# 64 bytes more between the contraction tiles of an expert's x, in a two-layer encoder trunk on one core

## The reference

```python
def moe_swiglu(h, w_router, w_gate_e, w_up_e, w_down_e):
    logits = (xt @ w_router).astype(jnp.float32)
    top_val, top_idx = lax.top_k(logits, TOP_K)          # TOP_K = 2 of 8
    gates = jax.nn.softmax(top_val, axis=-1)
    ...
    hg = lax.ragged_dot(xs, w_gate_e, sizes)             # 1024 -> 3584, by expert
    hu = lax.ragged_dot(xs, w_up_e, sizes)
    ys = lax.ragged_dot(jax.nn.silu(hg) * hu, w_down_e, sizes)   # 3584 -> 1024
    ys = ys * gates.reshape(-1)[order][:, None].astype(ys.dtype)
    out = jnp.zeros_like(xt).at[tok].add(ys)
```

## Time and profile before

| | us |
|---|---|
| median of 3 runs | 3622.34 |
| lowest, highest | 3621.78, 3625.7 |
| span of the profiled execution, first to last instruction | 3620.2 |
| TensorE busy in it | 3532.9 |
| DVE busy | 1803.5 |
| ACT busy | 1539.2 |

### The profile page before, as it was taken

How to read it: one execution, slowest core, us unless ns; L and a number is a source line. 1 busy time by engine, 2 the same in 40 slices (tenths; PEclk the granted TensorE clock), 3 DMA queues, 4 the chain that set the end, 5 groups by cost and what they waited for, 6 DMA issues and landing times. The chain is left out here.

```text
span 3620.2 us, 65480 instructions
## 1 busy us (share of the span) xinstructions
PE 3532.9 (98%) x24184; PEld 3219.3 (89%) x24184; DVE 1803.5 (50%) x2599; ACT 1539.2 (43%) x2207; POOL 205.3 (6%) x207
## 2 busy tenths in 40 slices
PE   8999899999999999979999999999999999999997
PEld 7888798888888889879899898998999999999997
DVE  5455543333333454465565565555655545545544
ACT  3445433332333342355454554544545444434433
POOL 1000000000000000040010010100100000000100
PEclk9999999999999999989999999999999999999999
DMA  5111332333223332256575565655655545544543
GB/s 190 37 49 39 140 94 93 93 93 117 93 93 99 121 95 67 101 190 220 184 236 193 193 230 186 231 186 190 231 194 194 191 157 177 193 162 158 183 159 124
DMA packets 158035, 540.68 MB, mean 149 GB/s; under 512 B 23480, under 2 KB 23520, under 8 KB 157920
## 3 DMA queue, kind: packets, MB, share of 16 engines
q1 hardware_dynamic: 129440, 467.72, 39.8%
q0 software_dynamic: 23872, 62.99, 5.0%
q10 hardware_dynamic: 4608, 8.39, 0.6%
HBM read 515.54 MB, written 45.48 MB: 155 GB/s over the span
## 5 line engine op out<-in xcount | busy, mean ns | idle before, releaser
L302 DVE TENSOR_TENSOR wl<-wraw,wh 128x1024 fp32r<-128x1024 f32 x884 | 1082.5, 1225 | 1322.0 <-ACT wh L298 1321.1
L298 ACT ACTIVATE wh<-wraw 128x1024 fp32r<-128x1024 f32 x884 | 934.2, 1058 | 1148.7 <-PE ps L315 1146.3
L315 PE MATMUL ps<-exh,wh 128*128 128x240 f32 (+3 forms) x3584 | 1019.3, 284 | 6.7 <-DVE wl L302 5.9
L315 PE MATMUL ps<-exl,wh 128*128 128x240 f32 (+3 forms) x3584 | 1018.8, 284 | 0.0
L315 PE MATMUL ps<-exh,wl 128*128 128x240 f32 (+3 forms) x3584 | 1018.7, 284 | 0.0
L315 PE MATMUL ps<-xs,wh 128*128 128x256 f32 (+1 forms) x3840 | 827.7, 323 | 2.4 <-DVE qAl L743 2.0
L315 PEld LDWEIGHTS ps<-exh,wh 128*128 128x128 f32 x3584 | 677.2, 189 | 7.4 <-issue 7.2
L315 PEld LDWEIGHTS ps<-exl,wh 128*128 128x128 f32 x3584 | 675.3, 188 | 0.2
L315 PEld LDWEIGHTS ps<-exh,wl 128*128 128x128 f32 x3584 | 675.2, 188 | 0.0
L315 PEld LDWEIGHTS ps<-xs,wh 128*128 128x128 f32 x3840 | 589.2, 188 | 76.2 <-issue 8.5
L315 PE MATMUL ps<-xs,wl 128*128 128x256 f32 (+1 forms) x1920 | 517.0, 321 | 0.0
(11 more groups left out here) (318 smaller groups left out, 3395.1 us busy)
## 6 DMA issues: line engine op xcount, KB each, us to landing
wraw<-in_w_expert SPq DMA_DIRECT2D x676, 512.0 KB, 3.3
wraw<-in_w_main SPq DMA_DIRECT2D x208, 512.0 KB, 3.5
hT<-in_xT POOLq DMA_DIRECT2D x2, 2048.0 KB, 10.1
h_d<-hT POOLq DMA_DIRECT2D x2, 2048.0 KB, 10.0
hT<-h_d POOLq DMA_DIRECT2D x2, 2048.0 KB, 13.9
xrow_d<-rows ACTq DMA_DIRECT2D x16, 256.0 KB, 2.0
hrow_d<-rows ACTq DMA_DIRECT2D x16, 256.0 KB, 3.9
yraw<-y_d POOLq DMA_DIRECT2D x4, 768.0 KB, 7.7
```

The lines of the kernel that those rows point to most:

```text
L298: act.activation(wh[:, j], wraw[:, j], ACT.Copy).then_inc(hi_done, 1)
L302: dve.tensor_tensor(wl[:, j], wraw[:, j], wh[:, j].bitcast(F32), ALU.subtract).then_inc(lo_done, 1)
L315: mm = pe.matmul(out[:, s], a, b[:, s], start=first and part == 0 and c == 0, stop=last and part == 2 and c + w == n)
```

## The change

The step from one contraction tile to the next of `exh` and `exl` grows by 16 floats (64 bytes) to 1600 bytes. The writes of ACT and DVE name columns 0 to 383 of it, as before. What lies behind the two tiles, and what the router keeps behind the items' tiles, moves up by 1024 bytes; the sets still fit. The whole diff:

```diff
--- before.py
+++ after.py
@@ -34,6 +34,7 @@
 NE = 8
 NG = 8
 CAP = 384
+SKEW = 16
 WIDTHS = (240, 256, 288, 304, 336, CAP)
 PIECES = -(-T // CAP)
 NCAND = PIECES * NE
@@ -171,7 +172,7 @@
         s3.close()
 
         s4 = ExitStack()
-        sb("under_items", [P, 2 * CAP + 2 * KD * CAP + 2 * F_EXP // P * CAP], F32, s4)
+        sb("under_items", [P, 2 * CAP + 2 * KD * (CAP + SKEW) + 2 * F_EXP // P * CAP], F32, s4)
         below = sb("below", [P, P], F32, s4)
         tokf = sb("tokf", [P, NT, 2], F32, s4)
         tokb = sb("tokb", [P, NT, 2], BF16, s4)
@@ -229,7 +230,7 @@
 
         s5 = ExitStack()
         mst = sb("mst", [P, 2, CAP], F32, s5)
-        exh, exl = (sb(n, [P, KD, CAP], F32R, s5) for n in ("exh", "exl"))
+        exh, exl = (sb(n, [P, KD, CAP + SKEW], F32R, s5) for n in ("exh", "exl"))
         mah, mal = (sb(n, [P, F_EXP // P, CAP], F32R, s5) for n in ("mah", "mal"))
         on = sb("on", [P, CAP // P, D], F32, s5)
         fgb = sb("fgb", [P, 512], F32, s5)
@@ -1802,12 +1803,12 @@
         def turn_x_act(act, it, banks=XT, ks=range(KD)):
             for k in ks:
                 act.wait_ge(xt_mm, 8 * it + (k + 1))
-                act.activation(exh[:, k], bank(banks[k], CAP), ACT.Copy, scale=gains[:, 3, k:k + 1]).then_inc(x_hi, 1)
+                act.activation(exh[:, k, 0:CAP], bank(banks[k], CAP), ACT.Copy, scale=gains[:, 3, k:k + 1]).then_inc(x_hi, 1)
 
         def turn_x_dve(dve, it, banks=XT, ks=range(KD)):
             for k in ks:
                 dve.wait_ge(x_hi, 8 * it + (k + 1))
-                dve.scalar_tensor_tensor(exl[:, k], bank(banks[k], CAP), gains[:, 3, k:k + 1], exh[:, k].bitcast(F32),
+                dve.scalar_tensor_tensor(exl[:, k, 0:CAP], bank(banks[k], CAP), gains[:, 3, k:k + 1], exh[:, k, 0:CAP].bitcast(F32),
                                          ALU.mult, ALU.subtract).then_inc(x_lo, 1)
 
         NF_E = F_EXP // P
```

## The result

The kernel after takes 3628.75 us, the median of 20 runs (3626.28 to 3634.76), beside 3622.97 us for the kernel before (3621.38 to 3628.37) on the same chip. The profiled execution spans 3627.4 us against 3620.2 us.

What follows compares the result with a forecast made beforehand. TensorE's own matmul stream was taken to bound the kernel. Matmuls, writes, later tiles and everything before the items were each put at 0, summing to 0, so the forecast stayed at 3622.3 us, range 3605 to 3638 us.

Steps and rivals of the forecast that it cites:

- What bounds the kernel, and how to price it: TensorE, busy 98% of the span, ends last; a matmul's price comes from starts in a stretch, 112.0 ns for 240 columns.
- The residue doesn't set the price: Stepping exh and exl through residues of 512 bytes costs TensorE's gate and up matmuls 0 ns, on three readings.
- The first: Two 256-column items at the same addresses cost 117.8 and 113.3 ns, so an address can't tell them apart.
- The second: wsh's 128-column matmul at distance 0 takes 111.4 ns, so up to 240 columns weight loads hide the moving operand's place.
- The third: 512 columns cost 233.4 ns in the dense layer and 234 in down halves, so turning the distance round changes nothing.
- Placement and the two ports: By the skill's separate TensorE read ports no placement of exh could matter, sum zero; the forecast wasn't rested on it.
- Rival (b): In gate and up products, changing distance at each k breaks the rhythm: slower, 3636 to 3643 us; chance 0.16.
- one sign of recognition: 288-column steps following k with a period of 24 matmuls, named as something that would make the prediction wrong.
- Rival (c): Excess is an address conflict that eight distances spread: half of the 32 us bound, 3606 us; chance 0.12.
- Rival (a): Rhythm drawn anew without any address; large flips 3611 us (chance 0.04) or 3630.5 us (0.02), small ones count as no change.
- (d): Change does what it says: exh and exl share a residue per k, eight in all; no effect, within no change's 0.66.
- Writes, waits, later tiles at 0: ACT's and DVE's writes (bound 2 us each), TensorE's waits for exl and tiles moved 1024 bytes were to add 0.

Runs made afterwards that it cites:

- x_plus64: Kernel before with exh and exl begun 64 bytes later at the old step, distance 0 modulo 256 from the weights; ratio 1.001.
- x_dist16: Kernel before with exh and exl meant to lie 16 bytes from the weights modulo 256, in fact 32 after the allocator's rounding; ratio 1.0027.
- dist0: Kernel before with 64 bytes put behind wl, so xs, mah and others get distance 0, exh and exl staying at 192; ratio 0.9986.
- half256: Kernel before with tiles 4 to 7 of exh and exl begun 256 bytes further, distance modulo 256 unchanged; ratio 0.9998.
- b_again: The kernel before without an edit, profiled once more; ratio 1.0005.
- rest1024: Kernel before with exh and exl kept and only the later tiles behind them moved by 1024 bytes; ratio 1.0.
- m1_micro: Separate kernel running only TensorE's product loop, other engines idle, at distances in 64-byte steps and the change's step; 256 columns 113.3 to 120.0 ns.
- m2_fine: The same TensorE-only loop at 16-byte distances, 512 columns included, and behind varied transposes or matmuls; 512 columns 226.7 to 236.7 ns.
- lead1: Kernel before with one more 256-column matmul at the start of each 256-column item; ratio 0.9998.

## Why the prediction was right or wrong

**What bounds the kernel, and how to price it: right.** TensorE's stream sets the end, the waits didn't move, and counting starts in a stretch finds the large terms of the 5.7 us.

**"The residue doesn't set the price": wrong, and this is the step that failed.** Each of the three readings was true, and none carried the conclusion. The first (same addresses, two prices) shows that something besides the address matters; I read it as showing that the address doesn't. The two micro kernels have both effects: for 256 columns at 192 bytes 113.3 and 117.8 ns are possible, at 0 only 120.0 was seen. In the kernel `x_plus64` has 120.0 ns, at distance 0, in both items. The second (wsh at distance 0 keeps the pace) is one price of 128 columns at one distance; no run here moves them to another, so it couldn't carry the conclusion that up to 240 columns the place is hidden. The 240 columns moved from 112.0 to 112.2 ns, 0.8 us in all, to 112.8 in `x_dist16` and to 113.3 in two items of `dist0`; I had named any such move as what makes the prediction wrong. The third (distance 192 against 64, and the earlier trace rows) compared two points where 233.3 occurs at both; distance 0, the one that would have told, with 226.7 ns, occurs for no 512-column product of the earlier trace rows.

**Placement and the two ports.** The loop alone, with ACT and DVE idle, has the prices of exh and exl in the kernel to 0.1 ns, and the same 512 columns cost 226.7 to 236.7 ns by distance. The Trainium skill, page SBUF — State Buffer, section "Who interferes with whom", gives TensorE separate read ports for the moving operand and the weights and has it wait for no other engine. The second half agrees with these runs. What I drew from the first half, that a placement can't matter, doesn't.

**Rival (b), slower by a broken rhythm: right in sign and in one sign of recognition, wrong in mechanism and size.** The steps do follow k with a period of 24. But `half256` shows that a jump in address costs nothing by itself, and 21 us became 5.7. Its price was taken between rhythms at one distance; what the change does is to replace one distance's price by about the mean of four, and that is a loss only where the one was the best: 6.7 us in the second 256 item.

**Rival (c), faster by spreading a conflict: true for 288 and 304 columns, 0.5 and 0.4 ns, 1.8 us in all.** Not the 26 us of the wide forms' part of its bound: no distance seen brings 288 below 130.0 ns.

**Rival (a), a new rhythm.** One of its terms came: the first down half of the first 256 item, 0.7 us, is in the fast rhythm in after. In the items the rhythm isn't drawn by the execution, since before and after repeat their prices there. Elsewhere it can be: 144 matmuls near 1340 us had 117.8 ns in before and 113.3 in `b_again`, the same program, a matter of 0.6 us.

**(d), eight residues.** The tiles do begin at eight residues of 512 bytes, but of distances only four differ.

**Writes, waits, later tiles at 0: right**, the last shown by `rest1024`. Of what lies ahead of the items the prediction also said 0, and the two profiles differ there by 1.45 us, which stays in part open. The time of 3628.75 us lies 6.4 us above the forecast, inside its own range of 3614 to 3631 us and the whole one of 3605 to 3638 us, and 0.16% is below the 0.2% that I called no change. But twenty runs tell it from no change, and the forecast of 0 ns had the wrong reason: that the time came so near it is luck, since losses of 8.2 us and gains of 2.5 us nearly cancel, and the largest term hangs on the second 256 item having been in the fast rhythm.

## What to carry to other kernels

When two runs of one loop at the same addresses differ, that tells of a second cause and not that the addresses are without one; before a price is called independent of placement, measure it with TensorE alone over all distances, which takes one kernel. For a stream of float32r matmuls that each load their weights, put the operand with the most and the widest matmuls where its distance to the weights is cheapest (here 0 modulo 256 bytes for 512 columns, 192 for 256), and step through the distances only if the present one is worse than their mean. Take such a table as a forecast and not as a fact: it failed for weights of 128 and 112 columns in turn, and where two prices are possible it doesn't say which one a kernel gets. Check the addresses in the compiled program, since the allocator rounds.

## What the runs showed of the hardware

- The price of a float32r matmul with its own weight load depends on the distance between its moving operand and its weights within a partition, modulo 256 bytes: 226.7 to 236.7 ns for 512 columns, 113.3 to 120.0 for 256, 130.0 to 134.7 for 288, 136.7 to 140.0 for 304, 111.7 to 113.3 for 240, over the multiples of 16 bytes. At 4 and 8 bytes 256 columns took 123.3 and 126.7 ns. These are prices of `m1_micro` and `m2_fine`, with 128 columns of weights each. In `dist0` 512 columns at distance 0 took 226.7 ns over 128 columns of weights, but 233.3 in five of six down halves with 128 and 112 in turn. Why is open: the runs show the dependence, no cause below it.
- At some distances two prices or more are stable, 113.3 and 117.8 ns for 256 columns at 192 bytes, picked in the loop by how many transposes or matmuls stand ahead. In the full kernel the same 256 items are slow and fast in `b_again`, `rest1024`, `half256` and `lead1` as in before, but one stretch of xs took 117.8 ns in one execution of the kernel before and 113.3 ns in another. What picks them there wasn't found.
- Cut or uncut depends on it as well: 512 columns cost 233.3 ns uncut and twice 113.3 or 117.8 cut at 192 bytes, but 226.7 uncut and twice 120.0 cut at distance 0.
